# Recurrent stage of a two-block network: the inverse's levels run in two halves of four units on TensorE, ScalarE and VectorE

## The reference, cut to what matters

```python
def step(S, inp):
    d_t, k_t, v_t, kk_t, a_t = inp[:5]
    sa = jnp.einsum("bhvk,bhk->bhv", S, -kk_t)
    S = (S * d_t[:, :, None, :] + sa[..., None] * (kk_t * a_t)[:, :, None, :]
         + v_t[..., None] * k_t[:, :, None, :])
    out = jnp.einsum("bhvk,bhk->bhv", S, inp[5]) if emit else None
    return S, out
return lax.scan(step, state0, xs, reverse=reverse)
```

## Time and profile before

| what | value |
|---|---|
| median of 3 runs | 4003.11 us (3998.90 to 4003.67) |
| the profiled execution: its span | 3997.2 us |
| PE busy in the span | 3803.5 us, 95% |
| DVE, ACT, POOL busy | 2297.2, 886.4, 1159.2 us |
| the recurrent stage | about 2236 to 2913 us of the span |

### The profile page before, as it was taken

The page is one execution under the profiler, slowest core; times in us unless marked ns, Lnnn a source line. Parts: engine busy times, 40 slices in busy tenths (PEclk is TensorE's granted clock), DMA queues, the critical chain, the costliest instruction groups (busy, mean ns, idle before and its releaser), DMA issues.

```text
span 3997.2 us, 77236 instructions
## 1 busy us (share of the span) xinstructions
PE 3803.5 (95%) x33844; PEld 2814.0 (70%) x33844; DVE 2297.2 (57%) x3572; ACT 886.4 (22%) x1689; POOL 1159.2 (29%) x860
## 2 busy tenths in 40 slices
PE   8999999999999999999998888888899999999998
PEld 3588887758888855555555678778757888558445
DVE  4578715657564149936443355555426877662695
ACT  3312100010110020021013444444212222550102
POOL 0144544105445420001441422233013554103202
PEclk9999999999999999999999999999999999999999
DMA  2134223423342212101333311111202333211221
GB/s 81 59 129 151 92 85 127 174 110 137 142 151 87 64 53 63 42 29 64 121 99 127 135 45 44 40 36 36 82 15 77 103 107 104 77 37 56 74 63 53
DMA packets 196056, 336.93 MB, mean 84 GB/s; under 512 B 17040, under 2 KB 149136, under 8 KB 187280
## 3 DMA queue, kind: packets, MB, share of 16 engines
q1 hardware_dynamic: 192000, 321.59, 24.1%
q0 software_dynamic: 3728, 10.49, 1.0%
HBM read 285.91 MB, written 38.80 MB: 81 GB/s over the span
## 4 chain that ended last, share of the span: by engine, by line
PE 88%; DVE 5%; ACT 3%; issue 3%; DMA 1%; SPq 0%; POOL 0%; DVEq 0%; ACTq 0%
PE lin_ps L1025 66%; PE out_ps L1025 8%; PE sum_ps L1025 7%; PE lin_ps L1430 6%; ACT arena L1966 2%; DVE arena L2561 1%; PE sum_ps L1911 1%; DVE rstd L2548 1%; ACT L1966 0%; ACT std L1966 0%; ACT ring L1966 0%; DVE hn L2561 0%; DMA features<-arena 0%; DMA arena<-pos 0%; DVE xs L2556 0%
## 5 line engine op out<-in xcount | busy, mean ns | idle before, releaser
L1025 PE MATMUL lin_ps<-hn,ring 128*128 128x256 f32 (+1 forms) x3520 | 1000.3, 441 | 7.5 <-DVE hn L2561 4.4
L1025 PEld LDWEIGHTS lin_ps<-hn,ring 128*128 128x128 f32 x3520 | 667.2, 190 | 315.7 <-issue 249.2
L1025 PE MATMUL lin_ps<-arena 64*64 64x64 f32 (+5 forms) x10032 | 761.1, 261 | 66.5 <-issue 29.0
L1025 PE MATMUL lin_ps<-arena,ring 128*128 128x256 f32 (+1 forms) x3200 | 769.6, 395 | 11.0 <-DVE arena L3029 9.4
L1025 PEld LDWEIGHTS lin_ps<-arena 64*64 64x64 f32 (+2 forms) x10032 | 578.8, 145 | 180.0 <-issue 93.7
L1025 PEld LDWEIGHTS lin_ps<-arena,ring 128*128 128x128 f32 x3200 | 609.0, 191 | 135.2 <-issue 53.9
L2561 DVE SCALAR_TENSOR_TENSOR arena<-arena,vec 128x512 f32<-128x512 f32 (+2 forms) x491 | 384.5, 858 | 1.1
L1966 ACT ACTIVATE arena<-lin_ps 128x512 f32<-128x512 f32 (+3 forms) x375 | 191.0, 524 | 753.6 <-PE lin_ps L1025 722.3
L3516 POOL TENSOR_TENSOR arena<-ring 128x512 f32<-128x512 f32 x67 | 89.5, 1335 | 896.9 <-PE lin_ps L1025 529.8
L1025 PE MATMUL sum_ps<-arena 64*64 64x64 f32 (+1 forms) x7180 | 315.4, 224 | 32.1 <-issue 23.8
L3516 POOL TENSOR_TENSOR ring<-ring 128x512 f32<-128x512 f32 x67 | 102.9, 1535 | 732.2 <-PE lin_ps L1025 428.9
(11 more groups left out here) (279 smaller groups left out, 4880.1 us busy)
## 6 DMA issues: line engine op xcount, KB each, us to landing
ring<-w_up SPq DMA_DIRECT2D x32, 1024.0 KB, 5.9
ring<-w_down SPq DMA_DIRECT2D x32, 1024.0 KB, 5.2
arena<-w_mod SPq DMA_DIRECT2D x24, 1024.0 KB, 7.9
arena<-w_mod SPq DMA_DIRECT2D x12, 2048.0 KB, 7.6
features<-arena SPq DMA_DIRECT2D x64, 384.0 KB, 6.1
ring<-w_conv_in SPq DMA_DIRECT2D x16, 1024.0 KB, 5.7
ring<-w_attn SPq DMA_DIRECT2D x16, 1024.0 KB, 5.7
ring<-features SPq DMA_DIRECT2D x40, 384.0 KB, 3.4
```

The costliest lines, as they stand in the source:

```text
L1025: return pe.matmul(out, lhsT, rhs, start=start, stop=stop)
```

## The change

The order of the three engines changes, and no arithmetic. The eight units of a level become two halves `s = 0, 1` of four units. Each half of z and fz has its own PSUM columns (the halves lie in different banks), its own ScalarE copy and its own VectorE update of `F`. `E` is still updated for all eight units at once, ahead of `chain_m`. Further:

- z of level 1 of the next group is issued unit by unit between the ez products of level 5 (`last_ez_first_z`);
- z of level 3 has two units of the key-1 features between its units (`level_z_feature`), which level 2 had before;
- o of the last chunk lies within the first half of z of level 5 (`level_z_o`);
- both directions of u are issued ahead of the features or ends (`chain_u_features` and `chain_u_ends` go);
- on VectorE `mask_k(G, 1)` moves from the end of level 2 to the head of level 3, and the E update of level 5 moves behind `take_o`, `mask_b`, the bonus values and the pieces of `aside(G, 5)`; on ScalarE `take_k(G, 1)` moves between x and u of level 3;
- the bonus sums use the PSUM bank of the outputs and wait for it.

```diff
-        z_ps = lin_ps[:, 1, 0:512].rearrange("p (u t) -> p u t", u=UN)
-        fz_ps = lin_ps[:, 1, 512:1024].rearrange("p (u t) -> p u t", u=UN)
+        z_ps, fz_ps = [[lin_ps[:, 1, 512 * s + 256 * n:512 * s + 256 * n + 256].rearrange("p (u t) -> p u t", u=4) for s in range(2)] for n in range(2)]
...
-        spare_ps = lin_ps[:, 1, 512:1024]
+        spare_ps = out_ps[:, 0, :]
...
+            def last_ez_first_z(G, s):
+
+                await_ez(G, 5, s)
+                await_z(G + 1, 1, s)
+                for u in units_of(s):
+                    e = heads(ez_ps[:, u, :], zc[:, u, :], E_[G % 3][:, u, :])
+                    m = z_unit(G + 1, u)
+                if s:
+                    e.then_inc(ez_mm, 1)
+                m.then_inc(z_mm, 1)
...
                 for l in range(1, 5):
-                    level_z(G, l)
+                    for s_ in range(2):
+                        if l == 3:
+                            level_z_feature(G, l, s_, 1, 1)
+                        elif l > 1:
+                            level_z(G, l, s_)
                     if G:
                         chain_xo(G - 1, l - 1)
-                    level_fz_ez(G, l)
...
+                    for s_ in range(2):
+                        level_fz_ez(G, l, s_)
+                    if G:
                         chain_u(G - 1, l - 1)
+                    if l == 1:
+                        ready_k(G, 0)
+                        features(1, G, 0)
+                    elif l == 2:
+                        ready_k(G, 1)
+                        features(1, G, 1, 0, 2)
...
-            def take_z(G, l):
-
-                act.wait_ge(z_mm, 5 * G + l)
-                copy(zc, z_ps).then_inc(z_ev, 1)
+            def take_z(G, l, s):
+
+                act.wait_ge(z_mm, z_count(G, l, s))
+                copy(zc[:, 4 * s:4 * s + 4, :], z_ps[s]).then_inc(z_ev, 1)
...
+                for l in range(1, 5):
+                    if l == 3:
+                        mask_k(G, 1)
+                    for s_ in range(2):
+                        level_f(G, l, s_)
                     level_e(G, l)
-                    if G and l < 5:
+                    if G:
                         chain_m(G - 1, l - 1)
...
+                if G:
+                    take_o(G - 1)
+                if not last:
+                    mask_b(G + 1, 1)
+                if G % 3 == 2 and not last:
+                    bonus_values(G // 3 + 1, 0)
+                aside(G, 5)
+                level_e(G, 5)
```

More of the change, by code:

```diff
@@ L1606, in ready_k, with ends, features @@
                 pe.wait_ge(gram_dve, 6 * G + 2 + 2 * half)
-            def ends(G, after=0):
-                for u in range(after, UN):
+                pe.wait_ge(gram_act, 6 * G + 4 + half)
+            def ends(G):
+                for u in range(UN):
                     m = ends_unit(G, u)
                 m.then_inc(gram_mm, 1)
-            def features(key, G, half, after=0):
-                for u in range(4 * half + after, 4 * half + 4):
+            def features(key, G, half, lo=0, hi=4):
+                for u in range(4 * half + lo, 4 * half + hi):
@@ L1635, in level_fz_ez @@
[L1635 to L1649 removed]
+                    pe.wait_ge(f_ready, f_count(G, l - 1, s))
@@ new lines, in z_unit, with level_z, level_z_feature @@
+            def z_unit(G, u):
+                return crossed(z_ps[u // 4][:, u % 4, :], nq[G % 2][:, u, :], F_[G % 2][:, u, :])
+            def level_z(G, l, s):
+                await_z(G, l, s)
+                for u in units_of(s):
+                    m = z_unit(G, u)
+                m.then_inc(z_mm, 1)
+            def level_z_feature(G, l, s, key, half):
+                await_z(G, l, s)
+                for n, u in enumerate(units_of(s)):
+                    m = z_unit(G, u)
+                    if n == 0:
+                        features(key, G, half, 2 + s, 3 + s)
+                m.then_inc(z_mm, 1)
@@ L1808, in _ @@
                 aside(G, 5)
-                level_fz_ez(G, 5)
+                for s_ in range(2):
+                    if last:
+                        last_ez(G, s_)
+                    else:
+                        last_ez_first_z(G, s_)
             G = GROUPS - 1
@@ L3347, in _ @@
                 last = G + 1 == GROUPS
-                for l in range(1, 6):
-                    if l < 5:
-                        level_f(G, l)
-                    if G and l == 5:
-                        take_o(G - 1)
+                for l in range(1, 5):
+                    if l == 3:
+                        mask_k(G, 1)
+                    for s_ in range(2):
+                        level_f(G, l, s_)
                     level_e(G, l)
-                    if G and l < 5:
+                    if G:
                         chain_m(G - 1, l - 1)
-                    if l < 3:
-                        mask_k(G, l - 1)
+                    if l == 1:
+                        mask_k(G, 0)
                     if l == 3 and not last:
@@ L3360, in _ @@
                         start_f(G + 1)
[L3361 to L3364 removed]
+                    if l == 4 and not last:
+                        mask_b(G + 1, 0)
                     aside(G, l)
+                if G:
[6 more added lines that the diff above has]
+                level_e(G, 5)
             for c in range(4):
```

123 lines of the change are left out of this document (69 added, 54 removed).

## The result

The changed kernel takes 4007.9 us in the median of 13 runs (3998.4 to 4016.4), the kernel before 3995.9 (3988.3 to 4003.7, 13 runs beside them): the ratio is 1.0024, with a 95% interval of 1.0015 to 1.0033. The forecast was 3990.5 with a range from 3969 to 4006. The profiled execution took 4003.5 us with a span of 4001.6.

What follows compares the result with a forecast made beforehand. TensorE's instruction packets, 3.77 us each, were taken to bound some nine tenths of the recurrent stage. Terms +1.2 - 5.5 + 1.8 - 2.4 - 2.7 - 3 - 4 + 2 = -12.6 us gave 3990.5 us, range 3969 to 4006.

Steps and rivals of the forecast that it cites:

- first to second group: Seven junctions with an output mean: E update behind mask and mean starts fz 0.5 us later each; half counted, +1.8 us.
- the forecast's signs: Marks expected in the changed profile; here, fz of level 1 waiting some 2 us for VectorE in a pair's first group.
- third rival: Slower: E update last on VectorE delays fz at all 23 junctions by 0.5 us, +11.5 us, 4014.6; chance 0.10.
- hidden by half: At first-to-second junctions, only half of the 3.5 us loss was counted, because the next instruction packet is often later.
- z under ez: z of level 1 between ez of level 5: -5.5 us at 7 third-to-first junctions, -2.4 at second-to-third and two others.
- nine tenths of the stage by packets: Recurrent stage: 166 instruction packets at 3.77 us are 626 of 677 us, so array work saved there only becomes idle.
- first rival: Array time saved across the stage counts in full, about -35 us, 3968; under 3980 was given chance 0.14.
- Features under z of level 3: Two feature units between units of z of level 3 save 14.4 us of array time; -4 us counted.
- u apart: u no longer overlaps the features, in 4 levels and 23 groups: +9.2 us of array time; +2 us counted.
- The first group: Copying z by halves saves fz some 0.55 us of waiting in each of 5 levels there, -2.7 us.
- Added waits: 83 more places where one wait does not do, a third of an instruction packet, +1.2 us.
- The main claim: Instruction arrival limits TensorE in most of the recurrent stage; issue idle would be no smaller than 63 us, rather larger.

Runs made afterwards that it cites:

- E first: Changed kernel with the E update of level 5 moved back right behind the copy of the outputs: 3997.8 us, 0.9994 of the kernel before.
- z apart: Changed kernel with the level-5 E update moved back and z of level 1 issued after all ez products, not between them: 3991.8 us, 0.9985 of the kernel before.

## Why the prediction was wrong, step by step

**The failed step** is the one for first to second group, "+0.5 us each, 3.5 us. I count half, +1.8". It put the scalar operation at 0.42 us, from the earlier trace rows. That row was not a price but a remainder: GpSimd's operation happened to have 0.42 us left when it came. A step that moves the operation's start moves this remainder too, anywhere from 0.17 to some 1.8 us. It became 1.61. TensorE's wait there, for which the forecast's signs named some 2 us, was 2.95 to 2.98. Measured: +2.2 us at each of five junctions, 11 us together; undone alone (E first), -12 us; done alone in the kernel before, +13; the held-up operation alone gone, -14. The rest of the step's sum was right: where the clock stayed full, level 1 took 1.73 us more, and with the operation at 0.42 that would have been 0.54 (an estimate, 1.73 - 1.19). Of the other 2.5 us of the 11, 2.2 are the lower clock behind the long wait, which the forecast had nowhere. The forecast had the mechanism of its third rival, an E update last on VectorE with 4014.6, and gave it 0.10; it priced all 23 junctions there at 0.5 us and not five at 2.2. Of the seven junctions two were spared.

**Waits were taken to be hidden by half.** "The next packet is often the later one" does not hold for a wait that stops TensorE for 3 us: against E first, level 1 of the five groups lost 11.1 us and the whole groups 11.3, so nothing of it was hidden.

**z under ez, -5.5 and -2.4.** The size at the third-to-first junction was right, 0.68 for 0.78. Its cause was not: 0.13 of it is the interleaving, the rest the halves. The forecast also left out that the joined block waits for the inputs of both. And the run with z apart shows that nothing of the interleaving that can be told reaches the end of the stage. The forecast held its own rule, nine tenths of the stage by packets, against the first rival but not against these terms: 3.77 us a packet also bounds the groups behind the junction.

**Features under z of level 3, -4; u apart, +2.** Undoing the first changed 0.9985 to 0.9981, undoing the second to 0.9975. Neither step is over what can be told, and together they show no gain from either part.

**The first group, -2.7.** Its levels 2 to 5 took 19.4 us for 26.4, 7.0 less, and 6.6 to 7.7 less in every kernel with halves. Two parts were missed. One is a wait of TensorE for ScalarE of 3.63 us, the longest in the earlier trace rows. In the kernel before ScalarE copies the second half of the features only at 2245.43, and then loads a table (1.28 us) before it comes to z of level 3; in the changed order that copy stands behind z of level 3, the table is loaded from 2241.28 on, and TensorE's wait is 1.27 us. The other is the clock. Levels 2 to 5 of the first group, before and in the change:

```profile
2236.67:2263.11 26.44, 20.96 (x536) 18.50 (x530) 13.46 (x30) 11.96 (x20) 3.21 (x2) 0.81 0.04 15
```

```profile
2236.28:2255.71 19.43, 17.41 (x560) 15.00 (x555) 14.02 (x38) 12.22 (x24) 3.24 (x2) 1.00 0.09 35
```

The granted clock was 0.81 before and is 1.00 in the change. Nearly the same work keeps TensorE busy for 3.5 us less, and the wait of level 3 is 2.4 us shorter: 5.9 of the 7.0. How much of either the halves bring, and how much the features under z, was not separated.

**Added waits, +1.2.** 167 packets for 166, as forecast; what they cost was not measured apart.

**The packets.** The main claim holds, and better than it was used: issue idle was forecast to be no smaller, and rose by 21 us while the array's work fell by 22; 64 instructions fewer in a group gave 14 to 17 us where the array could give 6; 19 us of array time put back cost nothing. One reading in it was off. The packet of the earlier trace rows does not move in the idle of the earlier trace rows but just ahead of it: in the trace it starts at 2554.97 and takes 1.34 us, the idle begins at 2556.33, and TensorE goes on at 2557.83. The link between the two is close all the same. Each issue idle over 0.3 us in the stage, 69 before and 82 in the change, ends 2.1 to 2.9 us behind the start of a packet, 2.5 on average; idle that a semaphore ends lies anywhere from 0.1 to 5.7 us behind one. How much of the stage is bound so, "some nine tenths", is less certain: it is an average over three stretches, and six packets fewer gave 14 to 17 us, not 22.6.

## What to carry to other kernels

A short operation's record on VectorE is not its price while GpSimd runs: compare where both end, and if they end together, read the duration as what was left of the other, price it from 0.2 us to GpSimd's whole operation, and keep it off the path. Not every small operation is held up (the reciprocal was not), so look at the one that is to be moved. Where TensorE's idle ends every 128 matmuls without a semaphore, count instructions, not array time: here fewer instructions shortened the stage, and interleaving to fill the array did not. And an update that the next product waits for goes first on its engine; moving it behind work "that is done by then" needs that work's worst duration.

## What the runs showed of the hardware

- On VectorE a `tensor_scalar` on 128x12 took 0.17 us with GpSimd idle and up to 1.74 us behind a GpSimd operation of 1.8 us on SBUF; where it was held up it ended within 0.04 us of that one. A `scalar_tensor_tensor` with two inputs took 1.61 us alike. A reciprocal on 128x12 took its 0.22 us and a reduce from 128x768 to 128x12 its 0.94 us throughout.
- A stage's TensorE work could be changed between 557 and 576 us of busy time at the same number of instructions without a measurable loss; with 1536 instructions fewer the stage was 17.8 us shorter.
- Each longer idle of TensorE without a semaphore ended some 2.5 us behind the start of a packet of 256 instructions.
- Behind an idle of 2.98 us TensorE was granted 1.2 GHz, and a block of fz and ez, 64 matmuls in the trace, took 1.68 us instead of 0.94.
